# The first scale item loaded ahead of the tokens, a thin product in four column groups, and head masks one head ahead of their norms

## What is computed

```python
mod = silu(c) @ w_ada + b_ada                 # shift, scale, gate of both halves; c: 1 prompt row, 8 sample rows
h = rmsnorm(x, g_mix) * (1 + sc1) + sh1
qa, ka, va, fa, qb, kb, vb, rb, alr, ga, gb = split(h @ w_in)
logf = log_sigmoid(fa + b_f)                  # 8 heads; cumulative sums enter the logits
o_a = softmax(qa k^T * scale + cq - ck, causal) @ v        # prompt; samples: over cached k, v and the new ones
log_a = log_sigmoid(alr @ w_alpha + b_alpha) / 16
o_b, s_new = gla_recurrence(qb, kb, vb, log_a, s0)         # in chunks of 64 tokens
o_b = rmsnorm(o_b, g_gla) * silu(rb)
x = x + gt1 * ((sigmoid(ga) * (o_a @ w_branch[:512]) + sigmoid(gb) * (o_b @ w_branch[512:])) @ w_o)
h2 = rmsnorm(x, g_ffn) * (1 + sc2) + sh2
x = x + gt2 * moe(h2)                         # 32 experts, top 4, FF 1024
y = rmsnorm(x, g_final)
```

## Time and profile before

| | us |
|---|---|
| median of 3 runs | 1245.64 (1245.16 to 1246.57) |
| the profiled execution | 1247.54 |
| its span, first to last instruction | 1245.7 |
| TensorE busy | 1163.0 (93%) |
| VectorE busy | 328.1 (26%) |
| ScalarE busy | 176.0 (14%) |
| DMA traffic | 500.76 MB, mean 402 GB/s |

### The profile page before, as it was taken

The page is one execution under the profiler, slowest core; times in us unless marked ns, Lnnn a source line. Parts: engine busy times, 40 slices in busy tenths (PEclk is TensorE's granted clock), DMA queues, the critical chain, the costliest instruction groups (busy, mean ns, idle before and its releaser), DMA issues.

```text
span 1245.7 us, 15292 instructions
## 1 busy us (share of the span) xinstructions
PE 1163.0 (93%) x6044; PEld 583.8 (47%) x6044; DVE 328.1 (26%) x685; ACT 176.0 (14%) x348; POOL 48.2 (4%) x95
## 2 busy tenths in 40 slices
PE   7999999999999999898989989998998988899997
PEld 4788756688543443434343435344242424243333
DVE  3289975323221020111101111111021011103123
ACT  3133232200211100200020011002000200020102
POOL 1032122100000000000000000000000000000000
PEclk9999999999999999999999998999999999999999
DMA  9998999999799999999999999999999999999995
GB/s 341 358 370 312 377 355 372 405 406 369 295 406 429 428 427 427 429 429 428 428 429 418 428 427 404 429 428 428 426 428 428 428 429 428 429 428 428 421 417 207
DMA packets 72700, 500.76 MB, mean 402 GB/s; under 512 B 9049, under 2 KB 11171, under 8 KB 43836
## 3 DMA queue, kind: packets, MB, share of 16 engines
q1 hardware_dynamic: 65840, 478.38, 93.2%
q0 software_dynamic: 6576, 21.42, 4.8%
q10 hardware_dynamic: 220, 0.09, 0.0%
HBM read 496.48 MB, written 3.38 MB: 401 GB/s over the span
## 4 chain that ended last, share of the span: by engine, by line
PE 69%; DMA 24%; DVE 2%; ACT 2%; issue 1%; SPq 1%; DVEq 0%
PE ps L1083 23%; DMA ring<-in_w_d 16%; PE ps L520 12%; PE ps L1170 11%; DMA early<-in_w_d 8%; PE ps L1267 4%; PE ps L1024 4%; PE ps L425 3%; PE ps L869 2%; PE ps L934 2%; PE ps L967 2%; PE ps L477 1%; SPq L2548 1%; ACT oT L1583 1%; PE ps L1040 1%
## 5 line engine op out<-in xcount | busy, mean ns | idle before, releaser
L1083 PE MATMUL ps<-ring,zone 128*64 128x512 f32 x1488 | 414.2, 593 | 6.6 <-DMA ring<-in_w_gu 2.8
L1170 PE MATMUL ps<-ring,oT 128*64 128x512 f32 x784 | 237.5, 617 | 31.3 <-DMA ring<-in_w_d 18.2
L1083 PEld LDWEIGHTS ps<-ring,zone 128*64 128x64 f32 x1488 | 132.4, 137 | 221.6 <-issue 218.1
L520 PE MATMUL ps<-early,ring 128*128 128x264 f32 x640 | 150.7, 392 | 2.3 <-DVE early L1748 1.4
L2211 DVE TENSOR_SCALAR zone<-ps 128x1024 f32<-128x1024 f32 x14 | 17.1, 1224 | 477.8 <-PE ps L1083 455.4
L1170 PEld LDWEIGHTS ps<-ring,oT 128*64 128x64 f32 x784 | 72.8, 142 | 148.5 <-issue 125.2
L520 PEld LDWEIGHTS ps<-early,ring 128*128 128x128 f32 x640 | 120.5, 192 | 31.2 <-issue 8.9
L1083 PE MATMUL ps<-zone 128*64 128x512 f32 x284 | 114.8, 593 | 0.0
L1083 PE MATMUL ps<-early,zone 128*64 128x512 f32 x240 | 98.8, 593 | 0.0
L1560 ACT ACTIVATE ps<-zone 128x1024 f32<-128x1024 f32 x14 | 14.4, 1027 | 450.9 <-DVE zone L2211 450.9
L1083 PEld LDWEIGHTS ps<-zone 128*64 128x64 f32 x284 | 35.4, 137 | 75.0 <-issue 74.1
(11 more groups left out here) (405 smaller groups left out, 957.5 us busy)
## 6 DMA issues: line engine op xcount, KB each, us to landing
ring<-in_w_gu SPq DMA_DIRECT2D x93, 2048.0 KB, 26.9
ring<-in_w_d SPq DMA_DIRECT2D x45, 2048.0 KB, 22.2
zone<-in_w_gu SPq DMA_DIRECT2D x16, 2048.0 KB, 25.3
early<-in_w_gu SPq DMA_DIRECT2D x15, 2048.0 KB, 31.2
ring<-in_w_ada SPq DMA_DIRECT2D x12, 2048.0 KB, 12.3
ring<-in_w_in SPq DMA_DIRECT2D x18, 1024.0 KB, 11.5
early<-in_w_d SPq DMA_DIRECT2D x8, 2048.0 KB, 24.3
zone<-in_w_d SPq DMA_DIRECT2D x7, 2048.0 KB, 19.6
```

The source lines that it names most:

```text
L520: ins = pe.matmul(bank[0:width, 0:T], w[:, k, c0:c0 + width], hT[:, k, :], start=(k == 0), stop=(k == KT - 1))
L1083: ins = pe.matmul(ps[64 * j:64 * j + CAP, c, :], xg[:, k, 2 * par + j, :], rows, start=False, stop=(k == KT - 1), skip_group_check=True)
L1170: ins = pe.matmul(ps[64 * j:64 * j + CAP, 4 + c, :], hidT[:, k, j * CAP:(j + 1) * CAP], w[j][:, kk, c * 512:(c + 1) * 512], start=(k == 0) ...
```

## The change

Three edits. SyncE issues ada0 ahead of x, ScalarE takes SiLU of c right behind its two loads, and TensorE turns c, multiplies with ada0 and only then turns all eight blocks of x; VectorE's copies follow, with the variance formed behind the sixth. The thin product puts odd k into two more column groups (rows 64 and 96), and VectorE adds the two halves. In the attention stretch a third score buffer (rows_512) lets VectorE mask head s + 1 ahead of the norm of head s; a gate tile moves behind the first scores, so that its sigmoid on ScalarE falls between the exponentials of heads 0 and 1; the cached values V0 to V3 take steps 5 to 8; the pair products and the turn of the masked values move within the order, the last pair product between the two vb_tok products.

```diff
+        head_scores = [attn[:, 0, :], attn[:, 1, :], rows_512[:, 0:3 * P]]
...
-            pe.wait_ge(sig("x_tok"), 32)
-            turn_tokens(range(4))
             pe.wait_ge(sig("c_silu"), 1)
...
             vector_filled(ins, "cT")
-            turn_tokens(range(4, 6))
...
             from_vector("cT")
             modulate_half(0, 0)
-            turn_tokens(range(6, KT))
+            pe.wait_ge(sig("x_tok"), 32)
+            turn_tokens(range(KT))
...
             for k in range(KT):
-                pe.matmul(bank[0:HA, 0:T], w_f[:, k, :], hT[:, k, :], start=(k == 0), stop=(k == KT - 1),
+                row = 64 * (k % 2)
+                pe.matmul(bank[row:row + HA, 0:T], w_f[:, k, :], hT[:, k, :], start=(k < 2), stop=(k >= KT - 2),
                           skip_group_check=True)
-                ins = pe.matmul(bank[32:48, 0:T], w_alr[:, k, :], hT[:, k, :], start=(k == 0), stop=(k == KT - 1),
-                                skip_group_check=True)
+                ins = pe.matmul(bank[row + 32:row + 48, 0:T], w_alr[:, k, :], hT[:, k, :], start=(k < 2),
+                                stop=(k >= KT - 2), skip_group_check=True)
...
             from_scalar("v_tok2")
-            for _ in range(4):
+            for _ in range(3):
                 gate_tile()
-            for s in range(11):
-                if s == 6:
-                    cached_values(1)
+            for s in range(HA + 1):
...
-                if s in (0, 2):
+                if s in (1, 3, 4):
+                    modulate(4, ps[:, 7, :], [{1: 0, 3: 1, 4: 2}[s]])
+                if s in (0, 1, 2):
                     gate_tile()
-                elif s in (1, 3, 4):
-                    modulate(4, ps[:, 7, :], [{1: 0, 3: 1, 4: 2}[s]])
-                elif s in (5, 7, 8):
+                if s >= 5:
                     cached_values(s - 5)
+                if s in (3, 5, 7):
+                    pair_values((s - 3) // 2)
...
-                if s % 2 == 1 and 3 <= s < HA + 3:
-                    pair_values((s - 3) // 2)
...
+            values_to_tokens(0)
+            pair_values(3)
+            values_to_tokens(1)
             pe.wait_ge(sig("tri"), 5)
             pe.wait_ge(sig("qg_kg"), 2)
+            chunk_scores(0)
+            turn_values(0)
+            chunk_scores(1)
...
             dma(c_rows[1:9, :], c_sample, "c_rows")
+            act.wait_ge(sig("c_rows"), 32)
+            nc.scalar.activation(c_rows, c_rows, ACT.Silu).then_inc(sig("c_silu"), 1)
...
-            take_gates(4)
+            take_gates(3)
...
-                if s == 7:
+                if s == 6:
                     act.wait_ge(sig("al_rest"), 1)
                     nc.scalar.activation(d, d, ACT.Exp).then_inc(sig("al_exp"), 1)
-                if s in (0, 2, 7, 8):
+                if s == 0:
+                    take_gates(1)
+                if s in (1, 2, 7, 8):
                     take_gates(1, func=ACT.Copy)
...
-            take_tokens(range(4))
             give(V.tensor_copy(cT[:, :, 0:9], take("cT")[:, 0:9 * KT].rearrange("p (k c) -> p k c", c=9)), "cT")
-            take_tokens(range(4, 6))
+            take_tokens(range(6))
...
             V.tensor_scalar(rstd, ssq, 1.0 / D, EPS, ALU.mult, ALU.add).then_inc(sig("x_var"), 1)
+            take_tokens(range(6, KT))
...
-            take_tokens(range(6, KT))
...
-                V.tensor_copy(alrT, bank[32:48, 0:T]).then_inc(sig("alrT"), 1)
-                give(V.tensor_scalar(fT, bank[0:HA, 0:T], b_f_col[:, 0:1], None, ALU.add), "falr", then_read=True)
+                V.tensor_copy(fT, bank[64:64 + HA, 0:T])
+                chain(V.tensor_copy(alrT, bank[96:112, 0:T]))
+                V.tensor_tensor(alrT, bank[32:48, 0:T], alrT, ALU.add).then_inc(sig("alrT"), 1)
+                give(V.scalar_tensor_tensor(out=fT, in0=bank[0:HA, 0:T], scalar=b_f_col[:, 0:1], in1=fT,
+                                            op0=ALU.add, op1=ALU.add), "falr", then_read=True)
...
-                if h >= 2:
-                    dve.wait_ge(scalar_full, a_index[f"turned{h - 2}"])
-                sc = attn[:, h % 2, :]
+                if h >= 3:
+                    dve.wait_ge(scalar_full, a_index[f"turned{h - 3}"])
+                elif h == 2:
+                    dve.wait_ge(sig("v_stored"), 16)
+                sc = head_scores[h % 3]
...
-            for s in range(10):
-                if s < HA:
-                    head_mask(s)
+            head_mask(0)
+            for s in range(9):
...
+                if s in (3, 5):
+                    take_head_values((s - 3) // 2)
...
+                if s + 1 < HA:
+                    head_mask(s + 1)
+                if s < HA:
+                    head_norm(s)
+                if s == 7:
+                    take_head_values(2)
...
-            sp.dma_start(tok[:, 0:2, :], x_prompt[0].rearrange("(t p) d -> p t d", p=P)).then_inc(sig("x_tok"), 16)
-            sp.dma_start(tok[0:NS, 2, :], x_sample.rearrange("b s d -> (b s) d")).then_inc(sig("x_tok"), 16)
             for item in ITEMS:
                 load(item)
+                if item == "ada0":
+                    sp.dma_start(tok[:, 0:2, :], x_prompt[0].rearrange("(t p) d -> p t d", p=P)).then_inc(sig("x_tok"), 16)
+                    sp.dma_start(tok[0:NS, 2, :], x_sample.rearrange("b s d -> (b s) d")).then_inc(sig("x_tok"), 16)
```

More of the change, by code:

```diff
@@ L720, in turn_values, with values_to_tokens, chunk_scores @@
                 vector_filled(ins, f"o_past{group}")
+            def values_to_tokens(c2):
+                bank = scalar_bank()
+                for c in (2 * c2, 2 * c2 + 1):
+                    for h in range(HB):
+                        i, other = h // 2, 64 - 64 * (h % 2)
+                        c0 = (c % 2) * 256 + i * DV
+                        ins = pe.matmul(bank[other:other + 64, c0:c0 + DV], vbT[:, h, c * CH:(c + 1) * CH],
+                                        ident[:, :], start=True, stop=True)
+                scalar_filled(ins, f"vb_tok{c2}")
+            def chunk_scores(i):
+                banks, last = [vector_bank(), vector_bank(ahead=1)], [None, None]
+                for c in range(NCH):
+                    for f in range(2):
+                        half, other = slice(64 * f, 64 * f + 64), slice(64 - 64 * f, 128 - 64 * f)
+                        last[f] = pe.matmul(banks[f][other, c * CH:(c + 1) * CH], e_k[half, i * NCH + c, :],
+                                            e_q[half, i * NCH + c, :], start=True, stop=True)
+                for f in range(2):
+                    vector_filled(last[f], f"A{i}{f}")
             from_scalar("v_tok2")
-            for _ in range(4):
+            for _ in range(3):
                 gate_tile()
-            for s in range(11):
-                if s == 6:
-                    cached_values(1)
+            for s in range(HA + 1):
                 if s < HA and s % 2 == 0:
```

39 lines of the change are left out of this document (8 added, 31 removed).

## The result

| | before | after |
|---|---|---|
| median, measured side by side | 1246.54 us (1243.3 to 1250.63, 20 runs) | 1250.64 us (1248.63 to 1253.52, 20 runs) |
| ratio of after to before | | 1.0032, 95% interval 1.0023 to 1.0041 |
| span of the profiled execution | 1245.7 us | 1247.9 us |

The change makes the kernel slower by 0.32%, 4.0 us. The forecast was +0.7 us, 1246.3 us, no measurable change; 1250.64 us lies above its range.

The account below looks back on a forecast made before the run. The expert weight stream was taken to bound the end, shifted by TensorE's arrival. Head +1.4, thin product -1.75 and waits +1.1 gave +0.7 us, 1246.3 us for the median; own range 1243.5 to 1248.0, with rivals 1241.5 to 1249.0.

Parts of the forecast that it names:

- What bounds the kernel: Expert weight stream, DMA full from 334 us: the end moves one to one with TensorE's gain or loss ahead of 288 us.
- The head: Kernel start, ada0 loaded ahead of x: +1.4 us, between 0.7 and 2.2, with ends -1.0 and +4.8.
- early rise of the clock: Head, clock up soon after ada0's product: rstd ends at 20.3 us, 0.7 later than before.
- the case of all at 1.2 GHz: Head: rstd ends at 22.7 us, 3.1 later; the second scale product may then cost another 1.7.
- the middle case: Head, clock rising about when it did before (17.4 to 18.1 us): rstd ends at 21.8 us, 2.2 later.
- signs for being right: Profile checks: among them L452 near 9.8 us, first projection at 24 to 26, thin product 1.8 us, al_log wait under 1.
- rival (a): Head: TensorE stays at 1.2 GHz through the tokens into the second scale product; head +3.6, 1248.6 us, chance 0.18.
- the forecast's slow case: Head, all of it at 1.2 GHz: eight token tiles take 6.4 us, rstd ends 3.1 us later.
- The thin product: Products for f and alr from 56.15 us: four column groups side by side save 8 steps of 0.22, -1.75 us.
- rival (c): Thin product: the four column groups do not overlap, +1.75 us, 1248.0 us, chance 0.08.
- The attention edit: Attention stretch, 148 to 208 us: TensorE's waits go from 5.9 to 7.0 us on a hand-laid time line, +1.1 us.
- The cap: V6's last quarter lands at 207.8 us, TensorE wants it at 208.7; a gain over 0.9 us turns into a wait.

Follow-up runs that it names:

- e1: The kernel before with the head edit alone (ada0 ahead of x, SiLU early, all token tiles behind the first product); ratio 1.0041.
- e4: The changed kernel with its head undone, thin product and attention edit kept; ratio 1.0005 to the kernel before.
- e15: The changed kernel plus spare products of ones in TensorE's pauses, none among the token transposes; ratio 1.0008 to the kernel before.
- e2: The kernel before with the thin product in four column groups alone; ratio 0.9988.
- e3: The kernel before with the attention edit alone (third score buffer, masks a head ahead, TensorE's new order); ratio 1.0016.
- e11: The same kernel as e4, measured again on one chip with another kernel; ratio 0.9983 to the kernel before.
- e8: The kernel before with thin product and attention edit, but all four gate tiles ahead of the first scores; ratio 0.9971.

## Why the prediction was wrong, point by point

**What bounds the kernel: right.** From the first expert product to the end it is 917.6 us before, 918.2 after and between 916.7 and 918.2 in e1 to e4. The end moves with TensorE's arrival.

**The head: the step that failed.** The term "+1.4 for the head" was +3.88 at the first projection, because the forecast let the clock stay up once it had risen, and so put the rstd and the second scale product at their 2.4 GHz durations; the token blocks were too short besides. By its own sum for the early rise of the clock (+0.7, with 13.4, 4.0, 0.6, 1.2 and 1.1):
- The tokens start at 13.04, not 13.4: -0.4. The product began at 9.45 and x landed about 13.0; both estimates were good.
- Eight token blocks take 5.84 us, not 4.0: +1.8. The forecast halved 0.8 to "0.5 each". At 2.4 GHz a block takes 0.65 us (e15: 5.24 for eight at a clock that was up), at 1.2 GHz 0.85. So 1.2 of the 1.8 were a wrong scaling between rows, whatever the clock, and 0.6 the clock. The two blocks of 0.8 us in the earlier trace rows had the rise at 17.6 us in them; a row of tokens at the higher clock alone would have mended it, and there is none.
- From the last block to the rstd product 1.6 us, not 1.8: -0.2.
- The rstd product 1.74 us, not 1.1: +0.6.
- The second scale product 3.18 us, not 1.93: +1.25. The text said that it "may cost another 1.7" in the case of all at 1.2 GHz, and left it out of the middle case.

0.7 - 0.4 + 1.8 - 0.2 + 0.6 + 1.25 = 3.75 of the 3.88 (the rest is rounding). Of its signs for being right, the first projection at 24 to 26 us failed with it. The reason given for the low value, that a dense product now stands ahead of the tokens, was right in its first half: the clock rose at 14.5. It was wrong to conclude that it would stay up. Before, ada0's product stands between six blocks of tokens and the end of the head; after, eight blocks in a row stand between the product and the rstd and scale products, and a pause of 1.02 us follows them. The forecast asked when the clock rises and never when it falls again, although was a row of exactly that: a fall behind work that had been at 2.4 GHz. It also noted, under rival (a), that six us of token transposes had not raised the clock, and did not ask whether they would hold it.

**Rival (a)** was the nearest, in the price (+3.6; +3.88 measured) and in the second scale product at 1.2 GHz. Its way there was another: it had TensorE stay at 1.2 GHz through the tokens, while the clock was up from 14.5 to 17.9 us, over more than half of them. That its price came so close is partly luck, since the tokens cost 5.84 us against the 6.4 of the forecast's slow case. Its time of 1248.6 is 2.0 under the median; of this 0.9 is the base, since the 20 runs of before have a median of 1246.54 and not 1245.64. The rest is not accounted for: in the profiles the gated branches come 3.19 us late, the times are 4.0 apart. Its chance was put at 0.18 by the argument on the rise. The throttled default that the Trainium skill names ("TensorE: Matmul & The Clock Gate", Part 1) was weighed for the start of the warm-up alone; the runs show that the same rule had to be asked for every weak stretch behind it.

**The thin product: right.** 8 x 0.22 = 1.75 us were forecast; it spans 1.9 instead of 3.7 us, rival (c) falls. al_log's wait of 2.2 us went wholly (forecast: 1.6 of it). e2 measured 0.9988. (The time given for rival (c) adds up to 1248.1, not 1248.0, on the forecast's own border to "slower".)

**The attention edit: right in size.** The hand-laid time line gave 5.9 us of waits before and 7.0 after, +1.1. In the 75 us from 140 to 215, TensorE is busy 70.01 us before and 69.30 after: 4.99 and 5.70 us of rest, +0.7. By the way from the thin product to the gated branches, e3 had +1.35. The wait ahead of dec_max was 0.6 (0.8 expected), the one for a vector bank ahead of pair 3 1.1 (1.4), the chunk-side waits stayed. The 0.7 for the scalar bank were 0.4, the 0.6 and 0.75 ahead of two heads' probabilities 0.5 each. The two table loads took 1.28 us each with the ACTIVATE 1.30 and 1.29 behind, as in the earlier trace rows. The 2.66 us for a switch that the Trainium skill gives ("ScalarE: Activation LUTs", "What ACT_TABLE_LOAD costs") don't show in this stream. From the thin product to the gated branches the sum is 3.19 - 3.88 = -0.7 us, and -1.75 + 1.1 = -0.65 was forecast.

**The cap: there, but not fixed, and without effect here.** The forecast held V6's landing near 207.8 us and let through only 0.9 us of a gain. TensorE does start V6 at its landing when nothing else holds it up: the last quarter lands at 211.78 us in after, 207.91 in e3, 205.99 in e4 and 206.12 in e11, and the V6 products start 0.04 to 0.05 us behind it each time. PE's own wait for it is 0.16 us in after and 0.4 in e3; in e4 and e11 only the weight load (PEld) waits, 1.0 us, which puts V6 0.2 to 0.3 us later. But the landing itself moved: issued 1.3 us earlier in e4 (186.83 instead of 188.16), it landed 1.8 us earlier, in e8 (186.27) 3.5 earlier, at 204.30, and TensorE reached V6 at 205.18 without a wait, against 208.64 before. "An earlier issue moves the landing little" was argued from the share of 1.02 and not from a row.

**The sign.** +0.7 was a small sum of two larger terms of opposite sign, with an uncertainty of the head (-1.0 to +4.8) wider than either. The range cut the head's upper end, although one mechanism led there.

## What to carry to other kernels

When work is moved to the front of a kernel, ask of each stretch at which clock it will run, of its end as well as of its start: light work (transposes) and pauses of about 1 us in front of a dense product can cost that product its rate, 3.2 to 3.6 us instead of 1.9 here. A transfer put first delays the one behind it by its own bytes; look at what hangs on the second one (here x, which landed near 13.0 us instead of 7.05 behind the 2.1 MB of ada0, with the tokens, the squares and rstd) before you give the place to a load that nothing else waits for. And a small sum of large terms is no forecast of "no change": its range is that of the largest uncertain term.

## What the runs showed of the hardware

- Spare products of ones from 2.2 us on lifted the clock to 2.4 GHz at 5.2 to 8.4 us, against 13.1 to 18.4 us in kernels without them, but did not hold it over 24 token transposes in a row (fall at 17.8 and 18.9 us with the pauses closed, at 15.2 with one of 1.18 us ahead of them).
- The same program gives different clock records from run to run: in seven profiles with the head of before, three had a stretch at 1.2 GHz behind 24 us (thin product at 56.15, 56.84 and 56.55 us) and four had none (54.13 to 54.47). In the three the clock had risen at 17.6 to 18.4 us, in the four at 15.2 to 16.4. It is worth 2 us in the thin product's start. A second such place lies ahead of the expert stream, between 314 and 331 us, in nine of eighteen profiles (before had it: clock 0.83 in the stretch below, and the way from its product at 316.88 us to the first expert product took 11.2 us, the same way in after 9.6).
- Halving the clock does not double a transposed block of tokens: 0.65 us at 2.4 GHz and 0.85 at 1.2 GHz (the step from one VectorE copy to the next in after), while the scale product goes from 1.93 to 3.64 us.

The stretch of before at the second such place:

```profile
318.00:328.00 10.00, 10.00 (x73) 7.84 (x70) 5.10 (x33) 5.77 (x10) 0.00 (x0) 0.83 0.82 333
```
